# One relative-bias table, built forward instead of backward, through a 128 times larger scratch tensor in HBM

## The reference, cut to what matters

```python
DILATED_BRANCHES = ((128, 1), (512, 4), (2048, 16))
for window, dil in DILATED_BRANCHES:
    offs_np = dil * np.arange(window // dil + 1, dtype=np.int32)
    bias = rel_bias[jnp.asarray(t5_causal_bucket(offs_np))].T.astype(jnp.float32)
...
logits = jnp.einsum('bqhd,bqkhd->bhqk', qi, kg).astype(jnp.float32) * scale
logits = logits + bias[None, :, None, :]
logits = jnp.where(valid[None, None], logits, -jnp.inf)
```

## Time and profile before

| what | value |
|---|---|
| median of the runs | 1159.81 us (1158.79 to 1160.36) |
| the profiled execution | 1160.36 us |
| span of its trace | 1158.6 us |
| mean granted TensorE clock | 0.961 |
| TensorE matmul busy | 1068.7 us, 92% of the span |
| VectorE busy | 764.4 us, 66% |
| ScalarE busy | 719.0 us, 62% |
| GpSimd busy | 101.0 us, 9% |

### The profile page before, as it was taken

One profiled execution on the slowest core, in us unless ns is written; L12 is line 12 of the kernel. 1 busy time (PEld: TensorE's weight loads), 2 busy tenths in 40 slices (PEclk: granted clock), 3 DMA queues, 4 the chain that ended last, 5 costly groups with the idle time before them and its releaser, 6 DMA issues.

```text
span 1158.6 us, 17394 instructions
## 1 busy us (share of the span) xinstructions
PE 1068.7 (92%) x6140; PEld 892.2 (77%) x6140; DVE 764.4 (66%) x1295; ACT 719.0 (62%) x1230; POOL 101.0 (9%) x187
## 2 busy tenths in 40 slices
PE   5988989999999899699989999998979999999987
PEld 4876777999998787688767878876768777777866
DVE  4557565666665665465667888876755567788885
ACT  5465464444443543377569889855748469889854
POOL 9001500000000012000040000000010140000000
PEclk9998699999999899899999999999889999999999
DMA  9762014755663635101336999964511427999950
GB/s 296 255 191 73 1 37 129 216 181 182 191 190 118 218 96 193 72 1 37 134 140 238 327 338 334 335 209 146 168 50 37 172 104 251 340 335 341 333 180 37
DMA packets 104411, 209.24 MB, mean 181 GB/s; under 512 B 7656, under 2 KB 49488, under 8 KB 104080
## 3 DMA queue, kind: packets, MB, share of 16 engines
q1 hardware_dynamic: 101984, 204.04, 51.3%
q0 software_dynamic: 2064, 3.25, 1.0%
q10 hardware_dynamic: 288, 0.99, 0.2%
HBM read 207.19 MB, written 1.06 MB: 180 GB/s over the span
## 4 chain that ended last, share of the span: by engine, by line
PE 82%; DVE 7%; ACT 6%; issue 3%; DMA 2%; ACTq 0%; SPq 0%; DVEq 0%
PE bank L805 22%; PE bank L1526 16%; PE bank L1545 10%; PE bank L1197 8%; PE bank L1207 8%; PE bank L900 4%; PE bank L881 2%; PE bank L724 2%; PE bank L889 2%; PE bank L880 1%; DMA expert_w<-in_moe_w_up 1%; PE bank L2029 1%; ACT x_high L778 1%; PE bank L1567 1%; PE bank L1034 1%
## 5 line engine op out<-in xcount | busy, mean ns | idle before, releaser
L805 PE MATMUL bank<-weight_parts,x_high 128*128 128x512 f32 (+3 forms) x832 | 246.0, 381 | 24.4 <-issue 16.7
L805 PEld LDWEIGHTS bank<-weight_parts,x_high 128*128 128x128 f32 x832 | 155.6, 194 | 54.2 <-issue 22.9
L1526 PE MATMUL bank<-expert_high,block_high 128*128 128x256 f32 x560 | 183.7, 328 | 3.6 <-ACT block_low L1474 2.6
L1454 DVE TENSOR_TENSOR expert_low<-expert_w,expert_high 128x1024 fp32r<-128x1024 f32 x140 | 164.8, 1219 | 15.1 <-ACT expert_high L1447 15.0
L826 DVE TENSOR_TENSOR weight_parts<-ring,weight_parts 128x1024 fp32r<-128x1024 f32 (+3 forms) x108 | 121.0, 1140 | 77.0 <-ACT weight_parts L823 76.9
L823 ACT CAST weight_parts<-ring 128x1024 fp32r<-128x1024 f32 (+3 forms) x108 | 103.5, 984 | 102.9 <-PE bank L805 92.2
L1526 PE MATMUL bank<-expert_high,block_low 128*128 128x256 f32 x560 | 158.1, 282 | 0.0
L1526 PE MATMUL bank<-expert_low,block_high 128*128 128x256 f32 x560 | 158.0, 282 | 0.0
L805 PE MATMUL bank<-weight_parts,x_low 128*128 128x512 f32 (+3 forms) x416 | 157.5, 378 | 0.0
L1447 ACT CAST expert_high<-expert_w 128x1024 fp32r<-128x1024 f32 x140 | 140.1, 1052 | 26.6 <-DMA expert_w<-in_moe_w_up 26.4
L1545 PE MATMUL bank<-expert_w,junk 128*128 128x512 f32 x280 | 131.2, 592 | 0.0
(11 more groups left out here) (340 smaller groups left out, 1733.3 us busy)
## 6 DMA issues: line engine op xcount, KB each, us to landing
expert_w<-in_moe_w_gate SPq DMA_DIRECT2D x70, 512.0 KB, 5.8
expert_w<-in_moe_w_up SPq DMA_DIRECT2D x70, 512.0 KB, 7.4
expert_w<-in_moe_w_down SPq DMA_DIRECT2D x70, 512.0 KB, 5.6
ring<-in_w_ff SPq DMA_DIRECT2D x64, 512.0 KB, 3.8
ring<-in_w_in SPq DMA_DIRECT2D x16, 512.0 KB, 12.2
ring<-in_a_w_in SPq DMA_DIRECT2D x16, 512.0 KB, 4.7
ring<-in_ple_w_gate SPq DMA_DIRECT2D x16, 512.0 KB, 5.5
ring<-in_w_o SPq DMA_DIRECT2D x8, 512.0 KB, 5.0
```

Of the source, the lines that this page charges most:

```text
L805: mm = nc.tensor.matmul(bank[:, j["m"] % 4, 0:n], j["operand"][x][:, 2 * c + kk, at[0]:at[1]], weight_parts[:, number % PAIRS, w, kk * n:( ...
L1454: nc.vector.tensor_tensor(half_of(expert_low[:, b % DEPTH, 0:2048], j), half_of(expert_w[:, b % DEPTH, 0:2048], j), half_of(expert_high[:, ...
L1526: mm = nc.tensor.matmul(bank[:, 4 + b % 2, 0:256].rearrange("p (q n) -> p q n", q=2), x[:, b % 2, k, :], w[:, k], start=k == 0 and n == 0, ...
```

## The change: the bias row is turned round and copied 128 times

The constant table now holds the distances in falling order, so `bias_row` does too. `toep_dram` gets one copy of the row for each of the 128 partitions, 8 x 128 x 384 numbers, written by one DMA whose source has a step of 0 over the 128 copies. Partition p of `toep` is loaded from its own copy, at an offset that falls by one with each partition. The two loads are now 256 columns to places 128 to 383, then 128 columns to places 0 to 127. The bias is added with `toep` read forward.

```diff
-    d = np.arange(SPAN) - 128
+    d = 255 - np.arange(SPAN)
...
-    toep_dram = nc.dram_tensor("toep_dram", [HEADS_A * SPAN], F32).ap()
+    toep_dram = nc.dram_tensor("toep_dram", [HEADS_A * P * SPAN], F32).ap()
...
-                                                     in1=toep[:, x["head"], ::-1], op0=ALU.mult, op1=ALU.add)
+                                                     in1=toep[:, x["head"], :], op0=ALU.mult, op1=ALU.add)
...
-        pool.dma_start(toep_dram.rearrange("(h n) -> h n", h=HEADS_A), bias_row[:, :]).then_inc(toep_spread, 16)
+        pool.dma_start(toep_dram.rearrange("(h p n) -> h p n", h=HEADS_A, p=P),
+                       bias_row[:, :].unsqueeze(1).to_broadcast([HEADS_A, P, SPAN])).then_inc(toep_spread, 16)
         pool.wait_ge(toep_spread, 16)
-        for at, n in ((0, 256), (256, P)):
-            pool.dma_start(toep[:, :, at:at + n], bass.AP(toep_dram.tensor, 1, [[1, P], [SPAN, HEADS_A], [1, n]])
-                           ).then_inc(toep_ready, 16)
+        pool.dma_start(toep[:, :, P:SPAN], bass.AP(toep_dram.tensor, 127, [[SPAN - 1, P], [P * SPAN, HEADS_A], [1, 256]])
+                       ).then_inc(toep_ready, 16)
+        pool.dma_start(toep[:, :, 0:P], bass.AP(toep_dram.tensor, 255, [[SPAN - 1, P], [P * SPAN, HEADS_A], [1, P]])
+                       ).then_inc(toep_ready, 16)
```

## The result

The changed kernel takes 1177.68 us (median of 4 runs, 1175.21 to 1180.43) against 1160.09 us before: a ratio of 1.0148, 95% interval 1.0116 to 1.0180. That is 1.5% slower, 18 us above the forecast and outside its range. The profiled execution took 1174.97 us with a span of 1173.2 us, 14.6 us more than before.

What follows compares the result with a forecast made beforehand. It took TensorE, busy 92% of the span and holding 82% of the chain, as the bound. Bias, write, loads and traffic at 0 us each summed to 0, so it forecast the median again, 1159.8 us, range 1157.6 to 1162.0.

Steps and rivals of the forecast that it cites:

- The bias read forward: L980 in attention A: eight instructions at 558 instead of 553 ns, a gain of -0.04 us, that is none.
- The cheaper-DVE rival: Bias add on DVE: removing the step of -1 saves time; even L980 halved gives 1159.6 us; chance 0.03.
- The write to HBM: POOL's write at L1900: 1.57 MB, landing about 10 us (4.7 to 20.5) by eight engines, 0 us on the path.
- My two neighbours: Trace rows that priced the write: the old 12 KB write (75 us of engine time) and the table loads (82 us).
- the 0.52 us: Engine time of the old short write's 7 packets in a 0.1 us window, taken as 74 ns a packet.
- The traffic added: Weight chunks beside the 1.57 MB write: land in 10.0 us, inside 10.5 us of notice; 0 us, far end 1 us.
- The chunk to which I had given 10.5 us: Fourth chunk of `w_uq`, issued at 65.01 us and cast at 75.53: the shortest notice found after 45 us.
- The loads: Two table loads at L1903: table ready 8.7 us after the write lands, 17.4 us as upper end; 0 us.
- The waits behind the table: DVE wants the table at 110.97 us, ACT the write landed at 109.28; table ready about 65 us; 0 us.
- The slow write through one engine: Rival: POOL's write lands at 120.3 us, table at 129.0, 18 us too late for DVE; 1178 us; chance 0.03.
- The weight stream: Rival: expert-stage weight loads change speed as HBM places move; 1% is 3.3 us either way, 1163.1 or 1156.5; chance 0.07.
- The clock of attention A: Rival: granted clock after 110 us rises from half to full, saving 11 us, 1149 us; chance 0.01.

Runs made afterwards that it cites:

- forward_only: Kernel before with only the bias step turned from -1 to +1 (bias added in wrong order); 1161.62 us, ratio to before 0.9993.
- src_step1: Changed kernel with the write's source replaced by neighbouring partitions 0 to 7 of the constant table; 1173.56 us, one run.
- by_head: Changed kernel with its one write cut into eight, one per head, each reading a single partition; 1200.31 us, one run.
- src_step4: Changed kernel with the write's eight source partitions at 0, 4 ... 28 of the constant table; 1161.64 us, one run.
- wide_source: Changed kernel with the bias row made on all 128 partitions, each writing 8 copies; 1159.97 us, ratio to before 0.9989.
- wide_four: Changed kernel writing from 128 partitions, four times (three into HBM tensors nobody reads), 6.3 MB; 1161.46 us, ratio to before 0.9981.
- src_step2: Changed kernel with the write's eight source partitions at 0, 2 ... 14 of the constant table; 1164.76 us, one run.
- half_spread: Changed kernel with 64 copies per head, partition p reading copy p // 2, four loads each filling every second partition; 1161.63 us, ratio 0.9997.
- late: Changed kernel with the write issued only when the input projection's matmuls are done; 1170.43 us, ratio to before 1.0080.

## Why the prediction was wrong, point by point

*The bias read forward: right.* 552 ns against a forecast of 558, and forward_only shows no gain. The cheaper-DVE rival is out.

*The write to HBM: the step that failed.* I had priced it at 75 to 82 us of engine time, 10 us over eight engines, 20.5 at the far end. The number of engines was right, but the write took 33.4 us. From 46 to 78 us its queue held 0.463 x 16 x 32 = 237 us of engine time, 0.70 us for each packet of three rows:

```profile
q0 software_dynamic: 704, 1.58, 46.3%
```

My two neighbours could not show it. The short write reads one row from each partition, a few packets in a tenth of a microsecond; that this is too little to fill a path is my reading and was not tested. The loads write to all 128 partitions. Neither keeps eight neighbouring partitions busy, and I asked how many engines take part but never how many ways out of SBUF the eight partitions have. src_step1, 2, 4 and by_head show that this sets the rate; src_step4 and wide_source show that it sets all of the loss. By the Trainium skill, "SBUF — State Buffer", the same section "Door 1: The DMA port swizzle", partitions 0 to 7 reach two of the 16 ports. Two groups at the 27 GB/s of by_head would have given 1.57 MB / 54 GB/s = 29 us, an estimate close to the 33.4 us.

I also misread. The answer it comes from says that three of its 7 packets are under 512 bytes:

```profile
DMA packets 7, 0.01 MB, mean 62 GB/s; under 512 B 3, under 2 KB 7, under 8 KB 7
```

So four rows share the 0.52 us, 0.13 us each and not 74 ns. The same sum then gives 1024 x 0.13 = 132 us of engine time, 16.5 us over eight engines and 33 us at half speed. That far end would have met the measured time, but by luck: it halves the rate because weight chunks share the engines, and with the same chunks beside it the write of src_step4 landed after 11.4 us.

*The traffic added: wrong as a consequence, and in its own way.* This is the term of the sum that the loss belongs to: 0 us in the prediction, 14.6 us in the trace. I had put the write's 4.7 us of bytes ahead of one chunk and got 10.0 of 10.5 us of notice. That is the pace of 16 engines, while I had priced the write at 10 us on eight; with this, the sum is 5.3 + 10 = 15.3 us, and it would have warned me. The amount of bytes is the wrong measure: wide_four moves four times as many and costs nothing. What counts is how long the write lasts. In the runs that write while `w_in` is still loaded, the first chunk issued beside the write landed about when the write did: at 75.7 us beside a write that landed at 78.2 in the kernel after, 62.3 and 62.7 in src_step2, 64.1 and 63.4 in half_spread, 56.7 and 56.4 in src_step4, 101.8 and 101.6 in by_head. So a write that is over before the cast of that chunk, which began at 66.39 us in the kernel before, costs little or nothing, and one that lands at 78.2 us makes it late. Only in wide_four did the first chunk land earlier, at 58.8 us beside a last write that landed at 68.5. In the kernel after, the eight chunks issued from 48.6 to 76.5 us took 13 to 29 us to land, against 3 to 8 us and notices of 10.5 to 18.7 us before. I had also taken SP's issue as fixed at 0.37 us; it rose to as much as 6.26 us. The chunk to which I had given 10.5 us was issued at 76.53 us instead of 65.01, 1 us after its cast had begun in the kernel before, and landed 13.4 us later. Its cast came 14.45 us late, nearly the whole loss. src_step4 shows that a write near my price would have been harmless: it landed after 11.4 us and no cast waited.

*The loads: nearly right.* The table was ready 11.2 us after the write had landed, against 8.7 before, inside my 17.4. *The waits behind the table: right.* It was ready near 90 us, when DVE, itself late, wanted it at 125.6. The late kernel shows what those waits cost once they do end last.

*The rivals.* The slow write through one engine gave 1178 us, within 1 us of what was measured, but by another mechanism: it had the write landing at 120 us and DVE waiting for the table. The write landed at 78.2 us, on eight engines, and DVE did not wait for the table. The agreement is chance. The weight stream did not change its speed elsewhere: the two traces are 14.6 us apart at L980 and 14.6 us apart at the end. The clock of attention A stayed at half (0.50 from 130 to 140 us). On the way PE, short of work, was granted less too, as the windows of the kernel after show (in the same windows before it was busy for 7.72 and 10.04 us, at 0.91 and 0.93):

```profile
70.00:80.00 10.00, 2.65 (x11) 2.65 (x12) 1.26 (x2) 1.75 (x3) 1.48 (x2) 0.62 0.73 159
80.00:92.00 12.00, 6.12 (x38) 5.78 (x37) 6.83 (x9) 5.37 (x8) 0.32 (x1) 0.78 1.05 357
...
130.00:140.00 10.00, 10.00 (x36) 7.60 (x37) 7.59 (x20) 6.12 (x15) 9.38 (x22) 0.50 0.00 0
```

*What stays open.* It is open how an engine shares its time between the two queues. If it took one packet from each in turn, by_head would show as many weight packets as write packets in 55 to 65 us; it shows 12 to 80. Why SP's issue becomes long is open too: it came with the slow packets (4.36 us at most in half_spread, where it cost nothing) and not with busy engines as such (0.70 us at most in wide_four), and it was not tested by itself. How the 16 us of waiting divide between late issue and slow landing is therefore not settled. Nor do the runs say why a chunk lands no earlier than the slow write beside it, or where the 3 us between the profiled execution and the medians come from.

## What to carry to other kernels

Before pricing a DMA by its bytes, look at which partitions it touches: eight neighbours gave 52 GB/s, eight at a distance of four gave three times that, and all 128 landed the same bytes in 6.6 us. A slow transfer that nobody waits for is still not hidden when it holds engines that other transfers need; what it costs is read from the landings and the notice of those others. Here a short transfer of the same form said nothing about the rate of the long one, and its packets have to be sorted by size before they are used as a price.

## What the runs showed that I had not expected

- Source partitions 0, 16 ... 112 are no faster than 0, 2 ... 14 (0.37 and 0.33 us a packet), while 0, 4 ... 28 are (0.21 us).
- Fifteen or sixteen engines on one partition at a time move 27 GB/s, less than eight engines on eight neighbours (52 GB/s), and the weight chunk that came beside them took 50.6 us.
- The issue of a DMA on SP's queue can take 6.26 us instead of 0.37 us beside the slow write; beside four times the traffic at full pace it took 0.70 us at most.
- Writing 6.3 MB instead of 1.57 MB to HBM, all landed within 23 us, left the kernel's time unchanged, but left one chunk only 1.9 us before its cast.
